# State-space output matrices made round by round in the scan, and one buffer for each side of the reordering

## What is computed

```python
ab_re = mag * jnp.cos(li * dt); ab_im = mag * jnp.sin(li * dt)      # decay of each state
v_re = jnp.einsum('blgh,gph->blgp', uf, bb_re)                      # inputs into states
v_im = jnp.einsum('blgh,gph->blgp', uf, bb_im)
_, _, s_re, s_im = lax.associative_scan(_complex_affine_combine, (a_re, a_im, v_re, v_im), axis=1)
y = (jnp.einsum('blgp,ghp->blgh', s_re, c_re) - jnp.einsum('blgp,ghp->blgh', s_im, c_im)
     + d_skip.reshape(SSM_GROUPS, SSM_GROUP) * uf)
y = jax.nn.gelu(y.reshape(bsz, L, SSM_WIDTH)).astype(u.dtype)
return y * jax.nn.sigmoid(y @ w_glu)
```

## Time and profile before

| what | us |
| --- | --- |
| median of 3 runs | 3772.22 (3770.91 to 3781.7) |
| the profiled execution, its own time | 3772.27 |
| its span in the profile | 3770.5 |
| TensorE busy in it | 3351.4 (89%) |
| VectorE busy | 1994.3 (53%) |
| ScalarE busy | 930.6 (25%) |
| GpSimd busy | 294.9 (8%) |
| heads' projection, first matmul to last | 926.1 to 1055.2 |
| scan, first instruction to the next stage's first load | 1059.5 to 1271.1 |

### The profile page before, as it was taken

The page is one execution under the profiler, slowest core; times in us unless marked ns, Lnnn a source line. Parts: engine busy times, 40 slices in busy tenths (PEclk is TensorE's granted clock), DMA queues, the critical chain, the costliest instruction groups (busy, mean ns, idle before and its releaser), DMA issues. The chain is left out here.

```text
span 3770.5 us, 48109 instructions
## 1 busy us (share of the span) xinstructions
PE 3351.4 (89%) x19662; PEld 3016.3 (80%) x19662; DVE 1994.3 (53%) x2626; ACT 930.6 (25%) x1143; POOL 294.9 (8%) x327
## 2 busy tenths in 40 slices
PE   3999999997878599899899898899988977999787
PEld 3999999997866499899789788799988974555445
DVE  5566566564877134556246345645445536666236
ACT  3222222222223211121011001222133314444213
POOL 0000000000536000000000000000022001222100
PEclk9999999998988599999999999999989988999998
DMA  2322222322353423311311311411121330000221
GB/s 95 96 87 77 74 91 86 96 85 97 128 61 86 135 95 123 112 45 45 123 50 45 106 67 50 144 41 41 49 82 36 136 127 1 1 1 1 91 77 68
DMA packets 102120, 287.36 MB, mean 76 GB/s; under 512 B 13120, under 2 KB 31936, under 8 KB 101568
## 3 DMA queue, kind: packets, MB, share of 16 engines
q1 hardware_dynamic: 101952, 285.03, 23.4%
HBM read 221.00 MB, written 63.98 MB: 76 GB/s over the span
## 5 line engine op out<-in xcount | busy, mean ns | idle before, releaser
L756 PE MATMUL mixer_in_dense<-mix_z_high,mixer_in_whigh 128*128 128x348 f32 x1344 | 443.6, 330 | 11.3 <-POOL mixer_in_out L593 11.3
L756 PE MATMUL mixer_in_dense<-mix_z_high,mixer_in_wlow 128*128 128x348 f32 x1344 | 436.6, 325 | 0.0
L756 PE MATMUL mixer_in_dense<-mix_z_low,mixer_in_whigh 128*128 128x348 f32 x1344 | 435.8, 324 | 0.0
L1888 PE MATMUL joint_dense<-rst_norms_operand_b_high,joint_whigh 128*128 128x342 f32 (+2 forms) x1056 | 344.9, 327 | 18.2 <-DVEq L2005 10.1
L138 PE MATMUL up_psum<-rst_norms_operand_b_high,up_whigh 128*128 128x342 f32 x1056 | 341.1, 323 | 21.5 <-DVE up_wlow L262 21.5
L1888 PE MATMUL joint_dense<-rst_norms_operand_b_high,joint_wlow 128*128 128x342 f32 (+2 forms) x1056 | 341.7, 324 | 0.0
L1888 PE MATMUL joint_dense<-irst_norms_operand_b_low,joint_whigh 128*128 128x342 f32 (+2 forms) x1056 | 340.6, 323 | 0.0
L138 PE MATMUL up_psum<-irst_norms_operand_b_low,up_whigh 128*128 128x342 f32 x1056 | 339.7, 322 | 0.0
L138 PE MATMUL up_psum<-rst_norms_operand_b_high,up_wlow 128*128 128x342 f32 x1056 | 339.6, 322 | 0.0
L756 PEld LDWEIGHTS mixer_in_dense<-mix_z_high,mixer_in_whigh 128*128 128x128 f32 x1344 | 257.5, 192 | 13.1 <-POOL mixer_in_out L593 11.9
L756 PEld LDWEIGHTS mixer_in_dense<-mix_z_high,mixer_in_wlow 128*128 128x128 f32 x1344 | 256.7, 191 | 0.8
(11 more groups left out here) (548 smaller groups left out, 6906.0 us busy)
## 6 DMA issues: line engine op xcount, KB each, us to landing
mixer_in_wstage<-w_in SPq DMA_DIRECT2D x56, 512.0 KB, 4.7
mixer_in_mod_w<-w_mod SPq DMA_DIRECT2D x64, 384.0 KB, 3.6
first_norms_weights<-w_up SPq DMA_DIRECT2D x44, 512.0 KB, 3.5
down_side<-h SPq DMA_DIRECT2D x24, 512.0 KB, 4.2
h<-down_out SPq DMA_DIRECT2D x24, 512.0 KB, 2.9
first_norms_weights<-ab_w_in SPq DMA_DIRECT2D x20, 512.0 KB, 3.5
p<-mixer_in_out SPq DMA_DIRECT2D x16, 528.0 KB, 2.9
first_norms_weights<-w_down SPq DMA_DIRECT2D x16, 512.0 KB, 4.9
```

Source lines behind the costliest of these rows:

```text
L756: mm = pe.matmul(pd[s % 2][:, 0:W], a[n % 2][:, P * m:P * (m + 1)], z[x][:, m, W * b:W * (b + 1)], start=m == 0 and i == 0, stop=m == DT - ...
L1888: mm = pe.matmul(pd[s % 2][:, 0:wide], a[n % 2][:, P * k:P * (k + 1)], m, start=k == 0 and e == 0, stop=k == DT - 1 and e == 2)
```

## The change

The products "outer" are no longer all made in the heads' projection. A new function `outer_part` makes them for one round's 8 pairs and m powers at once, also in six operations. In the heads' projection only round 0 is made, in three parts (powers 0 to 3, 4 to 7, and 8) ahead of slots 11, 12 and 13, and "skip" moves to slot 15. The products of rounds 1 to 3 are made in the scan, by VectorE between `decays(n)` and `weights(n+1)`, and TensorE's `kernel(n+1)` waits for them (`outer_ready`). The powers and C are kept through both stages. `chunked` and `natural` get one buffer each, and SyncE loads a tile only when ScalarE has done with the one ahead of it.

```diff
+def outer_part(ch, tt, ca, re, im, cr, ci, n, nq, k, m, t1, t2):
+    pairs, shape = slice(nq * n, nq * (n + 1)), [P, nq, m, SG]
+    r, i = (v[:, k:k + m, pairs].rearrange("p k n -> p n k").unsqueeze(3).broadcast_to(shape) for v in (re, im))
+    a, b = (v[:, pairs, :].unsqueeze(2).broadcast_to(shape) for v in (cr, ci))
+    u, v = (w[:, :, :].rearrange("p a b -> p (a b)")[:, 0:nq * m * SG].rearrange("p (n k h) -> p n k h", n=nq, k=m)
+            for w in (t1, t2))
+    ch.inc(tt(u, r, a, ALU.mult))
+    ch.do(tt(v, i, b, ALU.mult))
+    ch.do(tt(ca[:, pairs, 0, k:k + m, :], u, v, ALU.add))
+    ch.inc(tt(u, i, a, ALU.mult))
+    ch.do(tt(v, r, b, ALU.mult))
+    ch.do(tt(ca[:, pairs, 1, k:k + m, :], u, v, ALU.subtract))
...
-                       (8, "coefficients", 0), (9, "reverse", 0), (9, "scaled_b", 0), (10, "negate", 0), (10, "outer", 0),
-                       (12, "outer", 1), (13, "outer", 2), (15, "outer", 3), (16, "outer", 4), (18, "outer", 5),
-                       (19, "outer", 6), (21, "outer", 7), (22, "outer", 8), (NS, "skip", 0)):
+                       (8, "coefficients", 0), (9, "reverse", 0), (9, "scaled_b", 0), (10, "negate", 0), (11, "outer", 0),
+                       (12, "outer", 4), (13, "outer", 8), (15, "skip", 0)):
...
-                            ch.do(ts(pw[:, 2, :, :], pw[:, 1, :, :], -1.0, None, ALU.mult))
+                            ch.inc(dve.tensor_copy(ends_re[:, :, :], pw[:, 0, :, :]))
+                            ch.do(ts(ends_im[:, :, :], pw[:, 1, :, :], -1.0, None, ALU.mult))
...
+                            outer_part(ch, tt, ca, ends_re, ends_im, cr, ci, 0, NQ, k, min(4, TAU + 1 - k), t1, t2)
...
-        a, b = ([ph.sb(f"{n}{j}", (P, T1)) for j in range(2)] for n in ("chunked", "natural"))
+        a, b = ([ph.sb(f"{n}{j}", (P, T1)) for j in range(1)] for n in ("chunked", "natural"))
...
+                def fetch(m):
+                    if m:
+                        sp.wait_ge(moved, m)
+                    sp.dma_start(a[0][:, :], t["y_chunks"][m]).then_inc(landed, 16)
...
                     if n:
                         put(2 * n - 2)
+                        fetch(2 * n - 1)
                         put(2 * n - 1)
                     for par in range(2):
                         sp.wait_ge(stored[par], 16 * TAU * (n + 1))
-                    for m in (2 * n, 2 * n + 1):
-                        sp.dma_start(a[m % 2][:, :], t["y_chunks"][m]).then_inc(landed[m % 2], 16)
+                    fetch(2 * n)
                 put(DT - 2)
+                fetch(DT - 1)
                 put(DT - 1)
...
                     pe.wait_ge(spread, n + 1)
+                    if n:
+                        pe.wait_ge(outer_ready, n)
...
                     for m in (2 * n, 2 * n + 1):
-                        act.wait_ge(landed[m % 2], 16 * (m // 2 + 1))
-                        if m >= 2:
-                            act.wait_ge(y_stored[m % 2], 16 * (m // 2))
+                        act.wait_ge(landed, 16 * (m + 1))
+                        if m:
+                            act.wait_ge(y_stored, 16 * m)
...
                     if n + 1 < ROUNDS:
+                        for k in (0, TAU):
+                            outer_part(ch, tt, ca, ends_re, ends_im, cr, ci, n + 1, NQ, k, TAU if k == 0 else 1, t1, t2)
+                        dve.sem_inc(outer_ready, 1)
                         weights(n + 1)
```

32 lines of the change are left out of this document (12 added, 20 removed).

## The result

The changed kernel takes **3799.35 us** in the median of five runs (3796.38 to 3805.66), against 3772.22 (3770.91 to 3781.7). The ratio is 1.0066, with an interval of 1.0050 to 1.0083: slower, by more than the 0.3% that can be told from no change. The forecast was 3777.2, the range ended at 3791. The time is outside it.

A forecast was written before the change was run, and what follows sets the result against it. Bounds: in the heads' projection, waits for VectorE's evacuations behind "outer"; in the scan, a chain of hand-overs. Terms -11.8+0.5+6.2+10.1 = +5.0 on the median 3772.22 gave 3777.2 us, range 3766 to 3791.

The forecast's parts named there:

- Heads' projection, -11.8: First stage: fewer operations on VectorE leave TensorE one 3.4 us wait, at slot 14; 11.8 us saved, bounds -16.9 and -8.3.
- Twelve operations, 9.1 us a round: Scan, VectorE: six operations of 1024 elements (7.4 us) and six of 128 (1.7 us) added in rounds 0, 1 and 2.
- Round 0 for nothing: Scan round 0: the 9.1 us fit in VectorE's 16.71 us of idle time ahead of `weights`; no cost.
- Round 1, "+0.5": Scan round 1: VectorE's states, 9.1 us later, use up 8.6 us of slack against TensorE's inputs; +0.5 us.
- The clock rival: Scan: waiting for states(1) drops the clock ahead of outputs(1), which costs 12.8 us more; 3790 us, chance 0.18.
- Round 2 hidden: Scan round 2: VectorE's states come at about 1201.8 at the latest, and ScalarE is later.
- GpSimd hidden: Scan: GpSimd's last table comes 11.3 us later, but the third trip of `turned_back(3)` waits for inputs anyway; nothing.
- ScalarE and SyncE, +6.2: Scan round 1: ScalarE waits for the second tile's load, so kernel_out(3) begins 6.2 us later, delaying all that follows.
- Tail, +10.1: End of the scan: tiles 5, 6 and 7 are loaded and copied one by one, 21.0 us for 10.9; +10.1 us.
- The port rule: Scan: each us of VectorE stops GpSimd a full us, not 0.62, states(3) 6.5 us later; 3783.7 us, chance 0.11.

The follow-up runs named there:

- with the clock kept: The kernel before with eight 128x512 matmuls into an idle bank between outputs(2) and TensorE's wait for states(3), nothing of the change; 3761.1 us, ratio 0.9965.
- The tables left out: Changed kernel with the wide operations behind VectorE's first turning-back trip, and GpSimd's two scan tables (rounds 2 and 3) left out; ran once, 3784 us.

## Why the prediction was wrong

The terms as measured in the two profiles: -10.0 for the heads' projection, +21.2 up to the first gelu of round 1, +3.1 up to that of round 2, +10.2 in the tail, against a forecast of -11.8, +0.5, +6.2 and +10.1.

- **Heads' projection, -11.8: right within its bounds.** The tail shrank by 10.0. TensorE's wait ahead of slot 14 came as forecast (3.39 us for 3.4). Powers 0 to 3 took 5.0 us (forecast 4.9), powers 4 to 7 6.9 (6.5), but power 8, of 128 elements, 5.5 (1.7): four of its six operations took 1.1 to 1.3 us each beside GpSimd's of 512 elements, and all take 0.29 in the scan's round 0, with GpSimd idle. TensorE waited 0.75 us for it.
- **Twelve operations, 9.1 us a round: exact** (six at 1.22, six at 0.29). Round 0 for nothing: right.
- **Round 1, "+0.5": this is the step that failed.** I had set the end of VectorE's states(1) against the end of TensorE's inputs(2), found 8.6 us of slack and used it up. But VectorE's round hands over more than its states: `v_used` comes already in the first trip. For that the slack was only 2.8 us, and 9.1 - 2.8 = 6.3 us of wait were to be expected (6.5 measured), but I never looked for it, because the waits of before showed none there. The row at 1126.83 would have said so, beside VectorE's first trip. The trace of before shows waits that exist, not slacks that are about to be used. Of the 21.2 us, 6.5 were the wait and 14.7 the clock behind it.
- **The clock rival had the mechanism, and the wrong place.** It expected the fall ahead of outputs(1), from a wait for states(1), at 12.8 us. The price was about that (14.7), but the fall came one hand-over earlier, in the middle of outputs(0). The rule that it was based on held: a stall of a few microseconds, then an outputs stage at 0.50 to its end. I gave it 0.18, though an idle stretch ahead of the outputs had cost the kernel before some 13 us in its profile, in round 3: outputs(3) took 30.7 us there, and 17.0 with the clock kept.
- **Round 2 hidden, GpSimd hidden: right.** Outputs(3) waited 6.43 us (6.44 before) and ran at half clock as before.
- **ScalarE and SyncE, +6.2: right as an event, too large as a term.** Kernel_out(3) slipped by 28.4 - 21.2 = 7.2 us; 4.1 of it were given back, so 3.1 stayed. (The load in the middle landed 5.4 us after its issue, where I had taken 4.4.) I had not seen that both banks would be full behind the wait, and in the changed kernel inputs(3) ran at full clock, which they had not before.
- **Tail, +10.1: right** (10.2 from the last gelu's landmark, 34.4 - 24.3).
- **The port rule** did not decide: VectorE waited for TensorE in round 3, not for GpSimd, whose last table ended 142.6 us after the start of the scan, against 134.9 before. That is 7.7 us later, where the forecast had 11.3 and this rule 18.2. Its last operation in the changed kernel:

```profile
1192.09 1.21 POOL L884 TENSOR_TENSOR s_w_im<-scan_pool_t 128x24 f32<-128x24 f32 x1
```

  The tables left out show the other side. Beside GpSimd a scan operation took 3.1 us instead of 2.36. The Trainium skill (SBUF — State Buffer, section "SBUF: two separate sides") has the one engine blocked for the other's whole instruction. The trace agrees that both are slowed. It can't tell a lock from a sharing, since recorded times may hold blocked time.

What stays open: where in a wait the clock falls. A wait of 3.00 us that every kernel has ahead of its inputs, in the turning, was followed by inputs at 0.50 and mostly a recovery, one of 1.86 us ahead of outputs(1) by nearly the whole stage at 0.50. And what sets the moment of the rise is open: between executions it moved by 2 us in the scan's first kernel stage, and the inputs of round 2 ran at 1.00 in the kernel before and at 0.50 with the single buffers alone, though the two kernels are alike up to there.

## What to carry to other kernels

Work that is put in front of a hand-over spends the slack of that hand-over, and a wait table shows only slacks that are already negative. So for each engine that takes on work, list every semaphore that it gives in that stretch, with the time at which the receiver asks for it, not the last one alone. And where a stage has been seen to stay at half clock behind a wait, price the wait as itself plus that whole stage at half clock, and the start of the next. If the wait can't be avoided, matmuls into an idle bank are worth trying: here they gave some 13 us in each of two kernels, and nothing in a third, where the next round's wait took back what they had saved.

## What the runs showed of the hardware

- **An outputs stage behind a wait doesn't raise the clock.** At full clock it holds 1.00 (79 matmuls in 12.0 us). Behind a wait it stayed at 0.50 for 17 to 31 us with TensorE busy all the time, in round 3 of all eleven kernels without matmuls in the wait, and behind each wait in the middle of outputs(0) and outputs(1); there it rose only in the kernel stage that followed. It is not so when inputs at 0.50 run straight into the outputs: the clock then rose within the first half microsecond or so, as in outputs(2) of the kernel before, whose inputs had run at 0.50 for 5.5 us:

```profile
1196.52:1197.10 0.58, 0.58 (x3) 0.43 (x3) 0.43 (x2) 0.00 (x0) 0.00 (x0) 0.63 0.00 0
1197.10:1205.20 8.10, 8.10 (x47) 6.24 (x46) 3.95 (x8) 1.00 (x2) 0.00 (x0) 1.00 0.00 0
```

  The Trainium skill (TensorE: Matmul & The Clock Gate, "Part 1: The HAM clock gate") has the clock rise after a sustained busy stretch. Behind a wait that doesn't hold here for the matmuls of this stage, two in three of which use 64 of the rows; whether that is the reason no run shows.
- **Eight 128x512 matmuls (7.1 us) into an idle bank held the clock** through a wait of 6 us, in four kernels.
- **GpSimd's small elementwise work costs VectorE over 6 us in a round of 39,** in operations stretched by a third or more.
- **One execution of a kernel differs from the next by up to 9 us ahead of any change:** slot 9 of the heads' projection began between 978.9 and 988.0 us in kernels that are alike up to there. A sum made against one profile can't be better than that.
